# A hybrid attention and state-space layer on one core: first inputs, weight preparation and the start of the late stage put in another order

## The reference

```python
q, k, v, g_attn, u, g_ssm = split(rmsnorm(x) @ w_in)           # one combined input projection
a = windowed attention (128 keys, sinks) of q, k, v             # 8 heads of 64
y = Re(C x) + D u,  x = scan of x[t] = lam * x[t-1] + B u[t]    # 32 groups of 16 channels, 64 complex states each
a = rmsnorm(a * silu(g_attn), attn_out_norm_w)
g = gelu(y);  s = g * sigmoid(g @ w_glu + b_glu)
s = rmsnorm(s * silu(g_ssm), ssm_out_norm_w)
return x + concat(a, s) @ w_out
```

## Time and profile before

| | us |
|---|---|
| median of three executions | 1787.84 (1785.18 to 1788.72) |
| the profiled execution | 1782.28, its span 1780.5 |
| PE busy | 1693.3 (95%) |
| DVE busy | 1182.7 (66%) |
| ACT busy | 623.3 (35%) |
| POOL busy | 343.6 (19%) |

### The profile page before, as it was taken

One profiled execution on the slowest core, in us unless ns is written; L12 is line 12 of the kernel. 1 busy time (PEld: TensorE's weight loads), 2 busy tenths in 40 slices (PEclk: granted clock), 3 DMA queues, 4 the chain that ended last, 5 costly groups with the idle time before them and its releaser, 6 DMA issues. The chain is left out here.

```text
span 1780.5 us, 24710 instructions
## 1 busy us (share of the span) xinstructions
PE 1693.3 (95%) x8604; PEld 1354.1 (76%) x8604; DVE 1182.7 (66%) x2652; ACT 623.3 (35%) x1630; POOL 343.6 (19%) x425
## 2 busy tenths in 40 slices
PE   6899999999999999799999999788889999999999
PEld 5677777777777777588888888455567888888886
DVE  7787888767878887585634335799674665456532
ACT  5454454535454544422111111345342222212200
POOL 2122222212222221100014451022111111111110
PEclk9999999989999999799999999898989999999989
DMA  6311112213321110335536518566664445535222
GB/s 228 123 63 63 63 69 81 69 35 129 125 68 63 51 39 21 101 94 109 105 89 126 137 46 132 165 221 203 175 139 138 140 104 127 153 113 136 92 92 68
DMA packets 197420, 191.16 MB, mean 107 GB/s; under 512 B 118064, under 2 KB 153520, under 8 KB 197296
## 3 DMA queue, kind: packets, MB, share of 16 engines
q1 hardware_dynamic: 191088, 184.56, 37.6%
q10 hardware_dynamic: 6208, 5.02, 0.9%
HBM read 131.81 MB, written 57.73 MB: 106 GB/s over the span
## 5 line engine op out<-in xcount | busy, mean ns | idle before, releaser
L1163 PE MATMUL ps_b<-b_WH,b_XH 128*128 128x512 f32 (+1 forms) x776 | 287.1, 370 | 0.7 <-issue 0.4
L1165 PE MATMUL ps_b<-b_WH,b_XL 128*128 128x512 f32 (+1 forms) x776 | 277.5, 358 | 0.0
L1164 PE MATMUL ps_b<-b_WL,b_XH 128*128 128x512 f32 (+1 forms) x776 | 277.1, 357 | 0.0
L1163 PEld LDWEIGHTS ps_b<-b_WH,b_XH 128*128 128x128 f32 x776 | 148.6, 191 | 28.7 <-issue 9.1
L1165 PEld LDWEIGHTS ps_b<-b_WH,b_XL 128*128 128x128 f32 x776 | 148.4, 191 | 21.7
L1164 PEld LDWEIGHTS ps_b<-b_WL,b_XH 128*128 128x128 f32 x776 | 149.1, 192 | 18.8
L1428 ACT ACTIVATE b_SM<-ps_b,b_small 128x128 f32<-128x128 f32 x256 | 113.7, 454 | 113.0 <-DVE b_small L1611 110.4
L1118 POOL TENSOR_TENSOR b_XL<-b_XT,b_XH 128x1024 fp32r<-128x1024 f32 x33 | 80.2, 2431 | 377.6 <-ACT b_XH L1362 326.7
L793 PE MATMUL ps_g<-w_X0H,w_nextH 128*128 128x464 f32 x320 | 122.3, 382 | 2.6 <-DVEq L845 2.6
L795 PE MATMUL ps_g<-w_X0H,w_nextL 128*128 128x464 f32 x320 | 120.0, 375 | 0.0
L794 PE MATMUL ps_g<-w_X0L,w_nextH 128*128 128x464 f32 x320 | 119.9, 375 | 0.0
(11 more groups left out here) (338 smaller groups left out, 3696.7 us busy)
## 6 DMA issues: line engine op xcount, KB each, us to landing
b_XT<-in_xb SPq DMA_DIRECT2D x33, 512.0 KB, 4.0
b_XR<-in_x SPq DMA_DIRECT2D x33, 512.0 KB, 4.7
w_XT<-in_xt SPq DMA_DIRECT2D x36, 464.0 KB, 6.9
l_X<-in_xr SPq DMA_DIRECT2D x32, 512.0 KB, 4.4
out_out<-l_OUT SPq DMA_DIRECT2D x32, 512.0 KB, 3.0
scr_gs<-e_TG SPq DMA_DIRECT2D x36, 232.0 KB, 2.0
scr_u<-w_ST SPq DMA_DIRECT2D x12, 696.0 KB, 12.9
g_U<-scr_u SPq DMA_DIRECT2D x64, 130.5 KB
```

Of the source, the lines that this page charges most:

```text
L1163: pe.matmul(bank[:, 0:c1 - c0], XH[b][:, k, :], WH[:, k, c0:c1], start=(k == 0), stop=False)
L1164: pe.matmul(bank[:, 0:c1 - c0], XH[b][:, k, :], WL[:, k, c0:c1], start=False, stop=False)
L1165: mm = pe.matmul(bank[:, 0:c1 - c0], XL[b][:, k, :], WH[:, k, c0:c1], start=False, stop=(k == KD - 1))
```

## The change

In the early stage `U` of pairs 0 and 1 is loaded in front of the last two stores of `u`, and the sample columns of both pairs are copied there. In the state-space stage SP, not ACT, loads the Toeplitz matrix of pair 0, as its first work; ACT executes one gelu on one column behind its preparation; the 20 weight pieces are spread as one for each of iterations 0 to 11, then 3, 3 and 2; POOL waits in each iteration p for `v_full` of p+2 and `CP` of p+3 ahead of its low parts; three pieces of `Y0` are loaded in the last iteration; `attention_part(1)` is done ahead of the barrier. In the late stage attention inputs are loaded, split and multiplied for tile t+3 (PE: t+2) where it was t+2 (t+1), with three `OUT` buffers; `attention_part(2)` stands between `glu(0)` and `glu(1)`; the high and low parts of block 1 are made ahead of the last two of block 0. The diff, cut where it repeats (the argument `act` became `e` in `load_toeplitz`, which moved out of ACT's function):

```diff
@@ early_projections, SP
-                    if s == ST - 1:
-                        sp.wait_ge(u_st[0], 16 * ST // 3)
-                        groups.load_u(sp, 0)
+                        if (s, m) == (ST - 1, 1):
+                            sp.wait_ge(u_st[0], 16 * ST // 3)
+                            for p in range(2):
+                                groups.load_u(sp, p)
@@ early_projections, ACT
-                            groups.sample_inputs(act, 0, USA)
+                            for p in range(2):
+                                groups.sample_inputs(act, p, USA)
@@ state_space
-        NW, W_FROM = 20, 2
+        NW = 20
         def weights_of(p):
-            return [n for n in (2 * (p - W_FROM), 2 * (p - W_FROM) + 1) if 0 <= n < NW]
+            return [p] if p < 12 else {12: [12, 13, 14], 13: [15, 16, 17], 14: [18, 19]}.get(p, [])
@@ state_space, SP
+                load_toeplitz(sp, 0)
                 sp.dma_start(NO[:], I["out_norm"]).then_inc(const_ld, 16)
-                groups.load_u(sp, 1)
                 groups.load_u(sp, 2)
...
-                for n in range(2):
+                for n in range(3):
                     load_weight(n)
...
-                    for n in weights_of(p + 1):
-                        if n >= 2:
+                    for n in weights_of(p + 2):
+                        if n >= 3:
                             load_weight(n)
                     if p == 12:
                         for t in range(2):
                             ahead.load(sp, t, P, t + 1)
-                    if p == HG - 3:
+                    if p == HG - 2:
+                        ahead.load_first(sp)
+                    if p == HG - 1:
                         sp.wait_ge(w_lo, NW)
                         for s in range(2):
                             sp.wait_ge(y_st[s], 64 * 6)
-                    if p == HG - 2:
-                        ahead.load_first(sp)
-                    if p >= HG - 3:
-                        ahead.load_y(sp, ahead.Y0, 0, p - (HG - 3))
+                        for cb in range(3):
+                            ahead.load_y(sp, ahead.Y0, 0, cb)
@@ state_space, POOL
                 for p in range(HG):
+                    if p + 2 < HG:
+                        pool.wait_ge(v_full, p + 3)
+                    if p + 3 < HG:
+                        groups.cp.wait(pool, tile(p + 3))
                     for n in weights_of(p):
                         low_weight(n)
@@ state_space, PE
-                for h in range(2):
-                    ahead.attention_part(pe, (WOH, WOL), 0, h, P)
+                for t in range(2):
+                    for h in range(2):
+                        ahead.attention_part(pe, (WOH, WOL), t, h, P)
@@ state_space, ACT
-                load_toeplitz(0)
-                groups.sample_inputs(act, 1, USA)
                 sample_copies(0)
-                load_toeplitz(1)
+                load_toeplitz(act, 1)
...
                 act.wait_ge(const_ld, 32)
+                act.activation(WARM[:], groups.ID[:, 0:1], ACT.Gelu_apprx_tanh).then_inc(warm, 1)
@@ late_projections
-        OUT = [sb(f"OUT{i}", [P, D]) for i in range(2)]
+        OUT = [sb(f"OUT{i}", [P, D]) for i in range(3)]
@@ late_projections, SP
                 load_y(1)
+                load_a(2)
                 load_gs(1)
...
-                        if t + 2 < NT:
-                            load_a(t + 2)
+                        if t + 3 < NT:
+                            load_a(t + 3)
@@ late_projections, ACT
                     tanh(j, 3)
+                    if j == 0:
+                        high_a(2)
+                        high_g(1)
                     split_s(j, 2)
                     split_s(j, 3)
...
                 steps(0)
-                high_g(1)
...
-                        if t + 2 < NT:
-                            high_a(t + 2)
+                        if t + 3 < NT:
+                            high_a(t + 3)
@@ late_projections, POOL
+                ahead.low(pool, 2, P)
                 add_up(0)
...
-                        if t + 2 < NT:
-                            ahead.low(pool, t + 2, rows(t + 2)[1])
+                        if t + 3 < NT:
+                            ahead.low(pool, t + 3, rows(t + 3)[1])
@@ late_projections, PE
+                glu(0)
                 for h in range(2):
-                    attention_part(1, h)
-                glu(0)
+                    attention_part(2, h)
...
-                            if 1 <= t < NT - 1:
-                                attention_part(t + 1, h)
+                            if 1 <= t < NT - 2:
+                                attention_part(t + 2, h)
@@ late_projections, DVE
                     gate(j, 3)
+                    if j == 0:
+                        low_g(1)
                     low_s(j, 2)
                     low_s(j, 3)
...
-                add_attention(0)
                 low_g(0)
+                add_attention(0)
                 steps(0)
                 add_attention(1)
-                low_g(1)
+                add_attention(2)
...
-                        if 2 <= t + 1 < NT:
-                            add_attention(t + 1)
+                        if 3 <= t + 2 < NT:
+                            add_attention(t + 2)
                         add_state(i, t)
```

More of the change, by code:

```diff
@@ L1802, in state_space @@
         END = sb("END", [P, HG, 2, 8])
-        NO = sb("NO", [P, KD])
+        NO, WARM = sb("NO", [P, KD]), sb("WARM", [P, 1])
         (WUH, WUL), (WOH, WOL) = W3
         STG = [ahead.Y0[:, i, :, :].rearrange("p t q -> p (t q)") for i in range(4)]
-        const_ld, halved, zeroed = groups.const_ld, sem("norm_halved"), sem("pads_zeroed")
+        const_ld, halved, zeroed, warm = groups.const_ld, sem("norm_halved"), sem("pads_zeroed"), sem("gelu_ready")
         p_ld, u_ld, cs_ld = groups.p_ld, groups.u_ld, groups.cs_ld
@@ L1827, in weight, with load_toeplitz @@
             return I["w_out"][k * P:(k + 1) * P, c], NO[:, k:k + 1], WOH[:, k, c], WOL[:, k, c]
-        NW, W_FROM = 20, 2
+        NW = 20
         def weights_of(p):
-            return [n for n in (2 * (p - W_FROM), 2 * (p - W_FROM) + 1) if 0 <= n < NW]
+            return [p] if p < 12 else {12: [12, 13, 14], 13: [15, 16, 17], 14: [18, 19]}.get(p, [])
+        def load_toeplitz(e, p):
+            e.wait_ge(kp_st[p % 2], 16 * (p // 2 + 1))
+            if p >= RM:
+                y_full.wait(e, tile(p - RM))
+            for g in range(2):
+                k = scr["kp"][p % RM, SG * g:SG * g + SG, :]
+                moved = bass.AP(k.tensor, k.offset + P - 7 * SG, [[SG, 8], list(k.ap[0]), [1, 256]])
+                e.dma_start(MALL[p % RM][:, g, :], moved).then_inc(m_ld[p % RM], 16)
         with nc.Block() as block:
@@ L1971, in sample_states @@
                     act.activation(S[p % 2][:, :, NC + 8:NY], groups.H0[:, p, :, :], ACT.Copy).then_inc(h_in, 1)
-                def load_toeplitz(p):
-                    act.wait_ge(kp_st[p % 2], 16 * (p // 2 + 1))
-                    if p >= RM:
-                        y_full.wait(act, tile(p - RM))
-                    for g in range(2):
-                        k = scr["kp"][p % RM, SG * g:SG * g + SG, :]
-                        moved = bass.AP(k.tensor, k.offset + P - 7 * SG, [[SG, 8], list(k.ap[0]), [1, 256]])
-                        act.dma_start(MALL[p % RM][:, g, :], moved).then_inc(m_ld[p % RM], 16)
                 def sample_copies(p):
@@ L2027, in _ @@
                     if p + 2 < HG:
-                        load_toeplitz(p + 2)
+                        load_toeplitz(act, p + 2)
                     if p + 3 < HG:
@@ L2149, in late_projections @@
         a_full, s_full, o_mid, o_out = ahead.a_full, sem("s_part_full"), sem("out_mid"), sem("out_summed")
-        o_st = [sem(f"out_stored{i}") for i in range(2)]
+        o_st = [sem(f"out_stored{i}") for i in range(3)]
         def samples(j):
@@ L2216, in store @@
                     sp.wait_ge(o_out, 2 * t + 2)
-                    sp.dma_start(O["out"][r:r + n, :], OUT[t % 2][0:n, :]).then_inc(o_st[t % 2], 16)
+                    sp.dma_start(O["out"][r:r + n, :], OUT[t % 3][0:n, :]).then_inc(o_st[t % 3], 16)
                 load_gs(0)
@@ L2234, in _ @@
                         store(t)
-                sp.wait_ge(o_st[0], 16 * 17)
-                sp.wait_ge(o_st[1], 16 * 16)
+                for o in o_st:
+                    sp.wait_ge(o, 16 * NT // 3)
             @block.scalar
@@ L2426, in add_attention @@
                     n, b = rows(t)[1], block_of(t)
-                    if t >= 2:
-                        dve.wait_ge(o_st[t % 2], 16 * (t // 2))
+                    if t >= 3:
+                        dve.wait_ge(o_st[t % 3], 16 * (t // 3))
                     dve.wait_ge(x_ld[t % 3], 16 * (t // 3 + 1))
@@ L2432, in add_attention @@
                         dve.wait_ge(a_full, 2 * t + h + 1)
```

(8 more changed lines are left out.)

## The result

The changed kernel takes **1793.33 us** (1787.85 to 1797.17, seven runs) beside 1787.84 (1783.59 to 1788.75) for the kernel before on the same chip: a ratio of 1.0037, 95% interval 1.0022 to 1.0053, so 6.6 us slower (3.9 to 9.5). The forecast of 1786.6 was 6.7 too low and on the wrong side; the range of 1777 to 1794.5 holds the time.

The account below looks back on a forecast made before the run. VectorE was taken to pace the state-space body, with TensorE gaps at its start and at the change of stage. 3.4 + 10.9 - 0.4 - 10.2 - 2.5 = 1.2 us gained: 1786.6 us, range 1777 to 1794.5.

Parts of the forecast that it names:

- part 1: Start of state-space stage: earlier inputs gain 3.4 us at the TI product of pair 3; late u stores lose 0.4.
- part 2: State-space body: one weight per iteration, GpSimd products held to start with TI; gain 10.9 us.
- part 3: End of state-space stage: last eight weights in iterations 12 to 14 delay ScalarE and TensorE; loss 10.2 us.
- part 4: Change of stage and late start: TensorE arrives last, attention_part(2) waits for add_attention(1) on VectorE; loss 2.5 us.
- the loop of 9.2 us: State-space body: ScalarE's cycle with one weight, Toeplitz issue, outputs and kernel-store landing, 9.2 us against VectorE's 9.14.
- rival B: State-space body: ScalarE never catches up, every product costs VectorE 1.2 us; 7.0 us slower, 1794.8 us; chance 0.20.
- Rival C: Late stage: add_attention(1) is free early, the 8.1 us gap and its slow stretch go; 12 us more, 1774; chance 0.04.

Follow-up runs that it names:

- e2: Kernel before with only the weight change: one an iteration, last eight in iterations 12 to 14, GpSimd's waits, Y0 loaded last; ratio 1.0057, 10.2 us slower.
- e3: Kernel before with only the late-stage change: three OUT buffers, attention one tile further ahead, attention parts 1 and 2 moved; ratio 1.0041, 7.3 us slower.
- e12: Kernel before with only attention_part(1) issued ahead of the change of stage; ratio 0.9992 (0.9977 to 1.0007), no difference.
- e4: Changed kernel, but attention_part(2) waits for o_mid of tile 0, whose PSUM bank it takes, not tile 1; ratio 0.9995 to the kernel before.
- e5: Changed kernel without its late-stage part: first inputs and weights moved, attention and output buffers as before; ratio 1.0009 to the kernel before, 1.6 us slower.
- e9: Changed kernel with the parameters of pair 4 loaded ahead of U and the tables of pair 2; ratio 1.0023 to the kernel before.
- e7: Changed kernel with U of pair 15 issued in SP's iteration 11 ahead of weights 15 to 17; ratio 1.0006 to the kernel before.
- e11: Changed kernel without any of GpSimd's new waits; ratio 1.0022 (1.0008 to 1.0036) to the kernel before.
- e1: Kernel before with only first inputs moved: U of pairs 0 and 1 loaded earlier, Toeplitz 0 on SP, early gelu; ratio 0.9986, 2.5 us faster.

## Why the prediction was wrong

The terms of the sum against the stages, each a difference of means over the kernels that share the old or the new code:

| term | predicted | measured | from |
|---|---|---|---|
| part 1, with its 0.4 lost | 3.0 gained | 1.8 gained | 29.0 (3 kernels) to 27.2 (7) |
| part 2 | 10.9 gained | 7.6 gained | 116.5 (4) to 108.9 (5) |
| part 3 | 10.2 lost | 10.7 lost | 18.8 (4) to 29.5 (4) |
| part 4 | 2.5 lost | 3.8 lost | 500.1 (4) to 503.9 (7) |
| sum | 1.2 gained | 5.1 lost | comparison: 6.6 lost (3.9 to 9.5) |

e2, whose start of the stage is another, is in neither mean of parts 2 and 3; with it they are 7.4 gained and 10.1 lost. The spread of the profiles leaves some 1 us open on each difference (an estimate), so only the 3.3 us of part 2 stand clear.

All four signs were right; three sizes were off in the same direction, and the forecast stood so near zero that this turned it.

- **Part 2 failed most, 3.3 us.** The step was "Each uncovered product slows VectorE by about 1.2 and so lets ScalarE catch up by about as much", after which eight products were priced at 0.3. Of the 3.3, 2.8 lie in the body itself (108.9 for 106.1), 0.5 in that the kernels with the old weights average 116.5, not 117.0. ScalarE never got ahead for good: in nine of eleven iterations the product began 0.5 to 2.7 us behind TI. In that stretch, 1150 to 1246 us, the kernel stores landed as taken (median 4.1 for 4.3), but ScalarE also waited for the parameters of a pair, which the loop of 9.2 us left out:

```profile
ACT g_BD L487 <- DMA g_PAR<-in_ssm_d: 3.5, 4, 1.5
```

  Over ten iterations the cycle was (1246.16 - 1148.10) / 10 = 9.8 us, 0.67 a product over 9.14. The two cycles whose product did begin with TI, those of pairs 3 and 9, took 9.14 us, so a covered product cost nothing; the eight others took 9.5 to 10.2, 0.83 for each late product. That is rival B's mechanism; its price of 1.2 was too high and mine of 0.3 too low. Before the change two products an iteration cost 1.65 us, 0.82 each, so a product costs the same in both kernels: the body is shorter because it holds 11 of them instead of 20 (9 x 0.82 = 7.4 us, an estimate, for 7.6 measured), not because GpSimd is held.
- **Part 1 failed by 1.2 us, by the clock.** Up to the outputs of pair 0 it came true: they began 18.5 us behind TI(0) (1140.28 - 1121.83), as forecast (1136.9 - 1118.44). That the parameters of pair 4 stay the limit was right, their landing of 6 us a little short (issued by 1132.0, in use at 1138.48). The step that failed is "I add 0.3 for a longer gap of TensorE": TI(3) stood 7.8 us behind those outputs instead of 5.7, 2.2 more, since `direct(0)` ran at the lower clock. The row of before had it at the full clock; e3 and e12, with the same start, did not, so the 5.7 was a fast case. The 0.4 us for the late `u` stores was not needed: the start shows no loss, 1118.4 on average over the nine kernels with the new order and 1120.8 over the four with the old.
- **Part 3 was right in size, by the wrong limit.** The step that failed is that `load_u(15)` "lands at about T + 9, still inside ScalarE's time". It was in use at T + 9.3 to T + 10.1 in e4, e5 and e9, at T + 12.0 in the changed kernel (T = 1256.34), and TensorE had waited 3.4 to 7.35 us for it. Behind it TensorE needs 4.8 to 5.9 us, in part at the lower clock, before ScalarE can take the outputs of 13: these began at T + 14.6 to T + 16.9 instead of T + 13.7, with ScalarE idle. ScalarE's second set of weights was done earlier than thought, at T + 9.5 to T + 12.1 instead of T + 13.7, since the first set ended at T + 0.4 to T + 1.0 (T + 2.6 in the sum) and the kernel store landed in 2.4 to 3.5 us instead of 4.3. The errors cancel. e7 shows the difference: 3.5 to 5.8 us were to be had by moving one load.
- **Part 4 was right in mechanism, short by 1.3 us.** The wait at L1759 for L2445 was 12.2 instead of 10.5 (12.1 in e3); I gave 10 with three sums on GpSimd beside it, but four products of `low_g(1)` alone took 6.86. Attention 1 ahead of the barrier costs nothing that can be measured (e12, which is in neither mean).
- **Rival C** (the late order fills the gap) was given 0.04 with "I find no way around it". For the change as made that holds. e4 shows that the way is one number in a wait.

## What to carry to other kernels

Work moved away from a busy stretch pays its price where it lands: list what is queued behind it there, loads above all, and ask which of them an engine waits for next. A wait should name the buffer that it needs; one for "everything up to the last" costs nothing until somebody moves a step in front of it (12.2 us here). Where TensorE waits, the matmuls behind may run at either clock, from one profile to the next of the same code (`direct(0)` 2.9 us in before, 4.6 in e12): price both, from rows. A gate brings nothing where something else comes later still: here ScalarE did.

## What the runs showed of the hardware

- The length of TensorE's wait does not tell whether the clock falls: after 1.49 us (e12), 2.35 us (e11), 2.84 us (e9) and 4.06 us (after) the granted clock fell to the lower level (0.50 to 0.57 in the stretches behind), after 2.17 us (before), 2.38 us (e1) and 3.16 us (e7, `direct` in the tail) it stayed at 1.00.
- VectorE's scan, which no row of before shows beside GpSimd, is held by a GpSimd product: 2.30 us for two instead of 1.27. The prediction took this from the Trainium skill (SBUF — State Buffer, Who interferes with whom), by which a VectorE instruction with two SBUF inputs contends with GpSimd; the trace agrees.
- The last load of a pair's parameters, 2 KB (L455), took 3.0 to 7.1 us to land in the changed kernel (median 5.1 from 1120 to 1240 us), about as long as the weight loads of 256 KB (medians 5.5 and 6.0). An early issue is what helps: in e9 the parameters of pair 4 were in use 8.6 us behind TI(0) instead of 16.7.
